# Moving a sample group's softmax one memory update earlier, and spreading its cached-value products, in a fused two-layer decoder trunk

## The chip, the core and the metric

One core of a Trainium2 chip runs the whole step in one launch. The metric is device time in microseconds (us), median over runs. The profile is one further execution, with times from the start of its span.

## The reference, cut to what matters

Two layers, each for 1024 prompt tokens and for eight samples with one new token each. Heads are of width 64: eight of group A (windowed attention), eight of group B (mLSTM matrix memory). The change touches the samples' attention over cached keys and values, three patterns of 129 positions each (128 cached, one new):

```
def dilated_gather_stats(q, k_all, v_all, window, dilation, buf_len):
    ...
    s = jnp.einsum('bthd,btjhd->bthj', q, kg) * (HEAD_DIM ** -0.5)
    m = jnp.max(s, axis=-1)
    e = jnp.exp(s - m[..., None])
    l = jnp.sum(e, axis=-1)
    o = jnp.einsum('bthj,btjhd->bthd', e, vg) / l[..., None]
    return m, l, o

def combine_by_denominators(stats):
    ...
    w = ls * jnp.exp(ms - M)
    return jnp.sum(w[..., None] * os_, axis=0) / jnp.sum(w, axis=0)[..., None]
```

The merge makes it one softmax over all 387 positions. Beside it stands the B heads' memory, updated chunk by chunk (128 tokens), for the prompt, and once for each sample:

```
def mlstm_chunk(carry, inp):
    ...
    num = iw[..., None] * jnp.einsum('bhvk,bhtk->bhtv', C, q) + jnp.einsum('bhts,bhsv->bhtv', sc, v)
    ...
    C_new = cw[..., None, None] * C + jnp.einsum('bhs,bhsv,bhsk->bhvk', ws, v, k)
```

After both come output norms, the output projection, the gated feed-forward part and the per-layer embedding.

## The kernel before, in words

Every engine has its own instruction stream, written out in order (sync, gpsimd, tensor, scalar, vector blocks). Semaphores join them: `wait_ge(*at(sem, value))` stops an engine's whole stream. No scheduler decides anything; what stands earlier runs earlier.

A layer begins with the combined input projection, done pair of heads by pair of heads (p = 0 to 7). Weights are split into a high and a low float32r part (ScalarE rounds `whi`, L1441; GpSimd subtracts `wlo` in sixteen pieces, `split`, L841), and every product is three matmuls (`three`, L888 to L890). Four pairs of A heads are attended first, while the next pair's projection fills TensorE. Then come the four **updates**, q = 0 to 3, one per pair of B heads. An update first turns q and k (`turn_qk`, L1007), broadcasts rows of gates (L1218, L1227), makes the decay matrix (VectorE L2247, ScalarE L1697), and then walks the chunks c = 0 to 7:

- TensorE: projection products of the next pair (`next_products`; none in q = 3), the state's increment (L1240), score products `kq` (L1172), output products (L1254, L1259).
- VectorE: `finish(c)` updates the state (L2287) and the output rows `yb` (L2291 to L2295); `prepare(c + 1)` weights keys and scores (L2273, L2277). In q = 3 `prepare` stands ahead of `finish`. TensorE's chunk c + 1 waits for both.
- ScalarE: evacuates projections, squares the outputs (L1647), gates of the output (L1638 to L1642). GpSimd: gates times outputs (`gated`, L860) and `split`.

At the end of an update TensorE turns the state (L1270) as soon as the last `finish` has updated it.

The samples' attention is threaded through. In q = 0 to 2 VectorE handles one of 24 groups of cached keys per chunk (`sample_keys`, L2312, L2313; group i is sample i // 3, pattern i % 3), from two key buffers in `kvb`; SyncE loads group i once group i - 2 is used (`load_keys`, L643, L644; a new sample's query row goes ahead of its first group). In q = 3 the sums are turned by TensorE (L1210), VectorE takes their maximum (`sample_max`), ScalarE the exponential (L1701), VectorE normalises (`sample_weights`), TensorE turns the weights back (`sample_turn`, L1180), and VectorE copies them to their places in `pZ` (`sample_turned`), which GpSimd has zeroed (L870). From chunk 3 on 24 value products (`sample_values`, L1191, each two instructions in the trace) run: 5, 5, 8 and 6 in chunks 3 to 6. Their values, 256 KB each, lie in the space of the spent hi part: 0 to 15 come in during q = 2 (`load_strips`, when each token tile's projection is done), 16 to 18 in q = 3 behind the samples' state (1 MB) and two blocks of weights (2 MB), 19 to 23 after a round trip of the output gates. A semaphore counts six values, so product 12 waits for values 12 to 17 and product 18 for 18 to 23. The samples' own memory (`memory_gates`, `memory_keys`, `memory_output`, `memory_update`) is VectorE's work in chunks 2 to 5 of q = 3, the first three normalised output tiles in chunk 6. TensorE then turns these tiles (L1155) and the output projection begins.

## Time and profile before

| | |
|---|---|
| median of 3 runs (lowest, highest) | 3229.04 us (3226.77, 3229.59) |
| profiled execution | 3227.93 us |
| its span | 3226.1 us |
| busy: TensorE, VectorE, ScalarE, GpSimd | 97%, 58%, 32%, 28% of the span |
| mean granted TensorE clock | 0.985 of full |
| last updates (q = 3) | about 578 to 634 us and 2167 to 2224 us |
| first updates (q = 0), chunks | about 407 to 446 us and 1997 to 2036 us |

The layers run one after the other, so each stretch appears twice. Busy time of TensorE counts its matmuls, whose ends are modelled. A wait of TensorE is lost time nearly everywhere, as the projection work behind it has to be done anyway.

### The profile page before, as it was taken

The numbers are of one execution on the slowest core, as the hardware profiler recorded it, in microseconds if no ns is written. First come the engines' busy times: TensorE is split into PE (matmuls) and PEld (weight loads), VectorE is DVE, ScalarE is ACT, GpSimd is POOL, SyncE is SP. The second block draws the span as 40 slices with busy tenths as digits, with TensorE's granted clock in tenths as the row PEclk, the third lists the DMA queues.
The fourth block names the chain that finished last, engine by engine and source line by source line (L and its number), as shares of the span: only waits on it lengthen the run. The fifth ranks groups of instructions, "written<-read, shape, count | busy, mean of one in ns | idle before, by whom it ended". The sixth has DMA issues, their size and how long they took to land.

```text
span 3226.1 us, 50829 instructions
## 1 busy us (share of the span) xinstructions
PE 3122.2 (97%) x19459; PEld 2854.5 (88%) x19459; DVE 1857.2 (58%) x4365; ACT 1028.8 (32%) x2117; POOL 891.9 (28%) x2029
## 2 busy tenths in 40 slices
PE   7999999899999999999999999999999999999999
PEld 7887777599999999999987777766999999999998
DVE  5676455755555555557477755557555555555663
ACT  4444345533111121115344433454321111111251
POOL 3111122405322333223322210332132324223231
PEclk8999999899999999999999999998999999999999
DMA  5211234612111111110221111346111111111111
GB/s 172 54 47 51 54 74 118 189 49 66 44 48 40 40 66 40 53 40 21 94 71 44 49 48 50 82 132 183 64 40 40 40 66 40 53 40 40 40 37 71
DMA packets 228570, 208.87 MB, mean 65 GB/s; under 512 B 36676, under 2 KB 207620, under 8 KB 226736
## 3 DMA queue, kind: packets, MB, share of 16 engines
q1 hardware_dynamic: 228328, 205.62, 21.3%
q8 instruction: 154, 2.52, 0.3%
q14 instruction: 88, 0.72, 0.1%
HBM read 173.96 MB, written 31.61 MB: 64 GB/s over the span
## 4 chain that ended last, share of the span: by engine, by line
PE 88%; DVE 7%; ACT 2%; issue 1%; POOL 1%; DMA 0%; SPq 0%; DVEq 0%; ACTq 0%
PE ps L888 25%; PE ps L890 24%; PE ps L889 24%; PE ps L1051 2%; PE ps L1022 2%; PE ps L1037 2%; PE ps L1191 1%; POOL wlo L841 1%; PE ps L1254 1%; PE ps L1172 1%; DVE lo L1899 1%; PE ps L1259 1%; PE ps L897 1%; DVE att L2068 1%; DVE att L2057 1%
## 5 line engine op out<-in xcount | busy, mean ns | idle before, releaser
L841 POOL TENSOR_TENSOR wlo<-raw,whi 128x128 fp32r<-128x128 f32 (+3 forms) x1952 | 857.6, 479 | 1835.4 <-ACT whi L1441 1404.3
L888 PE MATMUL ps<-hi,wlo 128*128 128x344 f32 x2880 | 927.8, 322 | 13.7 <-POOL wlo L841 8.1
L890 PE MATMUL ps<-hi,whi 128*128 128x344 f32 x2880 | 922.5, 320 | 0.0
L889 PE MATMUL ps<-lo,whi 128*128 128x344 f32 x2880 | 921.8, 320 | 0.0
L888 PEld LDWEIGHTS ps<-hi,wlo 128*128 128x128 f32 x2880 | 544.4, 189 | 16.1 <-POOL wlo L841 8.7
L890 PEld LDWEIGHTS ps<-hi,whi 128*128 128x128 f32 x2880 | 543.7, 189 | 0.0
L889 PEld LDWEIGHTS ps<-lo,whi 128*128 128x128 f32 x2880 | 542.9, 189 | 0.6
L888 PE MATMUL ps<-whi,lo 128*128 128x512 f32 (+3 forms) x1056 | 413.5, 392 | 4.9 <-POOL wlo L841 4.4
L890 PE MATMUL ps<-whi,hi 128*128 128x512 f32 (+3 forms) x1056 | 390.2, 370 | 0.0
L889 PE MATMUL ps<-wlo,hi 128*128 128x512 f32 (+3 forms) x1056 | 389.2, 369 | 0.0
L2471 DVE TENSOR_TENSOR X<-X,ps 128x344 f32<-128x344 f32 x528 | 268.5, 512 | 184.3 <-PE ps L890 182.5
L1794 ACT ACTIVATE wb<-wb 128x344 f32<-128x344 f32 x132 | 64.9, 492 | 964.8 <-DVE wb L2458 964.8
L888 PE MATMUL ps<-yhi,wlo 128*128 128x344 f32 x1056 | 339.9, 322 | 0.8 <-DVE X L2471 0.8
L890 PE MATMUL ps<-yhi,whi 128*128 128x344 f32 x1056 | 338.3, 320 | 0.0
L889 PE MATMUL ps<-ylo,whi 128*128 128x344 f32 x1056 | 337.4, 319 | 0.0
L888 PEld LDWEIGHTS ps<-whi,lo 128*128 128x128 f32 (+1 forms) x1056 | 196.9, 186 | 67.2 <-issue 28.2
L890 PEld LDWEIGHTS ps<-whi,hi 128*128 128x128 f32 (+1 forms) x1056 | 197.1, 187 | 26.6
L2450 DVE TENSOR_TENSOR wa<-ps,rstd 128x344 f32<-128x344 f32 x132 | 68.3, 517 | 258.6 <-PE ps L890 258.2
L889 PEld LDWEIGHTS ps<-wlo,hi 128*128 128x128 f32 (+1 forms) x1056 | 197.7, 187 | 20.2
L1441 ACT ACTIVATE whi<-raw 128x2048 fp32r<-128x2048 f32 (+3 forms) x106 | 188.1, 1783 | 49.0 <-DMA raw<-in_w_down 37.6
L888 PEld LDWEIGHTS ps<-yhi,wlo 128*128 128x128 f32 x1056 | 198.7, 188 | 1.5 <-DVE X L2471 1.3
L889 PEld LDWEIGHTS ps<-ylo,whi 128*128 128x128 f32 x1056 | 198.3, 188 | 0.2
(325 smaller groups left out, 3881.4 us busy)
## 6 DMA issues: line engine op xcount, KB each, us to landing
raw<-in_w_up SPq DMA_DIRECT2D x44, 1024.0 KB, 5.1
raw<-in_w_in SPq DMA_DIRECT2D x112, 256.0 KB, 4.3
raw<-in_w_down SPq DMA_DIRECT2D x22, 1024.0 KB, 4.9
kvb<-in_cache_win_k SPq DMA_DIRECT2D x48, 256.0 KB, 3.6
cache<-in_cache_win_v SPq DMA_DIRECT2D x42, 256.0 KB, 4.7
X<-x_scratch SPq DMA_DIRECT2D x4, 2064.0 KB, 12.6
raw<-in_w_out SPq DMA_DIRECT2D x8, 1024.0 KB, 8.8
raw<-in_w_ple_gate SPq DMA_DIRECT2D x8, 1024.0 KB, 5.2
```

The costliest lines, as they stand in the source:

```text
L841: pool.tensor_tensor(out=wlo[:, s, r], in0=raw[:, s, r], in1=whi[:, s, r].bitcast(F32), op=ALU.subtract).then_inc(w_split, 1)
L888: nc.tensor.matmul(out, a_lo, b_hi, start=first, stop=False)
L889: nc.tensor.matmul(out, a_hi, b_lo, start=False, stop=False)
L890: return nc.tensor.matmul(out, a_hi, b_hi, start=False, stop=last)
L897: mm = nc.tensor.matmul(ps[0:5 * NB, bank, 0:width], thin[:, a:a + 5 * NB], w_h, start=k == 0, stop=k + 1 == KT)
L1022: mm = nc.tensor.matmul(ps[:, 2 * e + a // 4, 0:(b - a) * P].rearrange("p (t n) -> p t n", n=P), q3[r, qb, :], k3[r, a:b, :], start=True, ...
L1037: mm = nc.tensor.transpose(ps[:, 4 + half, (kb % 4) * P:(kb % 4 + 1) * P], att[:, a:a + P], ident[:, :])
L1051: mm = nc.tensor.matmul(ps[HD * e:HD * e + HD, 6, 0:P], zt[:, p % 2, kb, zc:zc + HD], att[:, a:a + P], start=(kb == 0), stop=(kb == qb))
L1441: do(nc.scalar.activation(whi[:, s, 0:used], raw[:, s, 0:used], ACT.Copy), w_hi, wait=False)
L1794: do(nc.scalar.activation(w, w, ACT.Gelu_apprx_tanh), gelu_done, wait=False)
L2450: do(v.tensor_tensor(out=w[:, 2:CH + 2], in0=ps[:, s % 3, 0:CH], in1=rstd[:, col(c)], op=ALU.mult), gate_read)
L2471: do(v.tensor_tensor(out=x, in0=x, in1=ps[:, 5 + (24 * i + j) % 3, 0:CH], op=ALU.add), dn_read, wait=False)
```

## The change

1. Cached keys: twelve groups in q = 0 and twelve in q = 1, by the table `KEYS` (1, 2, 2, 2, 2, 2, 1, 0 in chunks 0 to 7); none in q = 2. SyncE's loads likewise, and value strips in q = 2 without keys between them.
2. The softmax moves to q = 2: turn of the sums and copy in chunk 0, maximum in 1, exponential in 2, weights in 3, turn back and copies in 6. TensorE waits behind both turns before its next `kq` (they share PSUM bank 0). Buffers `sm`, `zb`, `small` move to `kvb`, `pZ` to tiles 6 and 7 of lo with another layout (six copies instead of three), and GpSimd zeroes it after the first split of q = 2. The three reads of `zb` move from q = 3 to the start of q = 2.
3. Value products: two inside `turn_qk` of q = 3, four after the broadcasts, then 3, 2, 2, 3, 3, 3, 2, 0 in the chunks (table `VALUES`).
4. The samples' memory work starts one chunk earlier, its gate multiply stays in chunk 5.

```diff
-STRIPS = {2: (0, 1, 2), 3: (3,), 4: (4,), 5: (5,), 7: (6, 7)}
+KEYS = (0, 1, 3, 5, 7, 9, 11, 12, 12)
+def keys_of(q, c):
+    return range(12 * q + KEYS[c], 12 * q + KEYS[c + 1]) if q < 2 else ()
+VALUES = (6, 9, 11, 13, 16, 19, 22, 24, 24)
...
+        sm = kvb[0:HD, 0, 0:385]
+        pZ = lof[:, 6 * TOK:KT * TOK].rearrange("p (k n) -> p k n", k=2)[:, :, 0:6 * P]
...
-                    for i in range(max(2, NT * h2), NT * (h2 + 1)):
-                        load_keys(i)
-                        if h2 == PAIRS - 2:
-                            for t in STRIPS.get(i - NT * h2, ()):
-                                load_strips(t)
+                    if h2 < 2:
+                        for i in range(max(2, 12 * h2), 12 * (h2 + 1)):
+                            load_keys(i)
+                    else:
+                        sp.wait_ge(*at(kq_used, 3 * NB))
+                        for j in range(3):
+                            sp.dma_start(zb[:, j, :], Zd[j].rearrange("b (h d) -> (b h) d", d=HD)).then_inc(zb_in, 16)
+                        for t in range(NT):
+                            load_strips(t)
...
-                for j in range(3):
-                    sp.dma_start(zb[:, j, :], Zd[j].rearrange("b (h d) -> (b h) d", d=HD)).then_inc(zb_in, 16)
...
-                        pool.wait_ge(*at(gemm_done, GEMM_OUT))
-                        pool.memset(pZ, 0.0).then_inc(pz_set, 1)
...
                         split(B + n)
+                        if q + 2 == PAIRS:
+                            pool.wait_ge(*at(gemm_done, GEMM_IN + (NT + 1) * (2 * PAIRS - 1) + 6))
+                            pool.memset(pZ, 0.0).then_inc(pz_set, 1)
...
                             if half == 1 and j == 1:
+                                if p + 1 == 2 * PAIRS:
+                                    sample_values(0, 2)
...
                     next_products(done[2], ahead_b(q, 0))
+                    if q + 1 == PAIRS:
+                        sample_values(2, VALUES[0])
...
-                        if q + 1 == PAIRS and c == 2:
+                        if q + 2 == PAIRS and c == 0:
+                            pe.wait_ge(*at(kq_used, 3 * NB))
+                            for r in range(3):
+                                mm = nc.tensor.transpose(ps[0:HD, 0, (r + 1) * P:(r + 2) * P], ...)
+                            mm.then_inc(st_ready, 1)
+                        elif q + 2 == PAIRS and c == NT - 2:
                             sample_turn()
...
                         if q + 1 == PAIRS:
-                            sample_values(c)
+                            sample_values(VALUES[c], VALUES[c + 1])
                         elif c + 1 < NT:
+                            if q + 2 == PAIRS and c == 0:
+                                pe.wait_ge(*at(sp_max, 1))
+                            elif q + 2 == PAIRS and c == NT - 2:
+                                pe.wait_ge(*at(pj_done, 1))
                             kq(c + 1)
...
+                        if q + 2 == PAIRS and c == 0:
+                            sample_scores()
+                        elif q + 2 == PAIRS and c == NT - 2:
+                            sample_turned()
                         finish(c)
...
-                            sample_keys(NT * q + c)
-                        elif c == 0:
-                            sample_max()
+                            for i in keys_of(q, c):
+                                sample_keys(i)
+                            if q + 2 == PAIRS and c == 1:
+                                sample_max()
+                            elif q + 2 == PAIRS and c == 3:
+                                sample_weights()
```

**VectorE, first update, chunks 1 to 2.** `kvb<-kvb` with `att<-kvb` is one group of cached keys, `Cst` the state in `finish`. Before:

```order
L2312 TENSOR_TENSOR kvb<-kvb 128x512
L2313 TENSOR_REDUCE att<-kvb 128x8
L2287 SCALAR_TENSOR_TENSOR Cst<-Cst,cwb,ps 64x65 x2
L2291 SCALAR_TENSOR_TENSOR den<-ps,em 128x2
L2293 TENSOR_TENSOR den<-ps,den 128x2
L2294 RECIPROCAL den<-den 128x2
L2295 TENSOR_TENSOR yb<-ps,den 128x128
L2273 SCALAR_TENSOR_TENSOR att<-zt,att 128x128
L2277 SCALAR_TENSOR_TENSOR att<-ps,att 128x256
L2312 TENSOR_TENSOR kvb<-kvb 128x512
L2313 TENSOR_REDUCE att<-kvb 128x8
```

and changed:

```order
L2348 TENSOR_TENSOR kvb<-kvb 128x512
L2349 TENSOR_REDUCE att<-kvb 128x8
L2348 TENSOR_TENSOR kvb<-kvb 128x512
L2349 TENSOR_REDUCE att<-kvb 128x8
L2323 SCALAR_TENSOR_TENSOR Cst<-Cst,cwb,ps 64x65 x2
L2327 SCALAR_TENSOR_TENSOR den<-ps,em 128x2
L2329 TENSOR_TENSOR den<-ps,den 128x2
L2330 RECIPROCAL den<-den 128x2
L2331 TENSOR_TENSOR yb<-ps,den 128x128
L2309 SCALAR_TENSOR_TENSOR att<-zt,att 128x128
L2313 SCALAR_TENSOR_TENSOR att<-ps,att 128x256
L2348 TENSOR_TENSOR kvb<-kvb 128x512
```

A second group of keys now stands between `prepare` and the next `finish`.

**TensorE, opening of the last update.** `ident,zt` turns q and k, `ident,att` 64x128 turns the samples' sums, `rowr,ident` broadcasts, `rstd,kT` is `kq`, `cache,vectors` a value product. Before:

```order
L1270 MATMUL ps<-ident,Cst 64x128 x2
L1007 MATMUL ps<-ident,zt 128x128 x16
L1210 MATMUL ps<-ident,att 64x128 x3
L1218 MATMUL ps<-rowr,ident 64x512 x4
L1227 MATMUL ps<-rowr,ident 128x512 x4
L1172 MATMUL ps<-rstd,kT 128x128 x2
L1240 MATMUL ps<-zt,att 128x130
```

and changed, as far as the first chunk's products:

```order
L1295 MATMUL ps<-ident,Cst 64x128 x2
L1036 MATMUL ps<-ident,zt 128x128 x12
L1023 MATMUL ps<-cache,vectors 64x512 x2
L1036 MATMUL ps<-ident,zt 128x128 x4
L1232 MATMUL ps<-rowr,ident 64x512 x4
L1241 MATMUL ps<-rowr,ident 128x512 x4
L1023 MATMUL ps<-cache,vectors 64x512 x4
L1201 MATMUL ps<-rstd,kT 128x128 x2
L1256 MATMUL ps<-zt,att 128x130
L1201 MATMUL ps<-rstd,kT 128x128 x2
L1275 MATMUL ps<-zt,att 128x65 x2
L1280 MATMUL ps<-Cst,att 128x130
```

Six value products now stand in the opening, and the turn of the sums has left it.

## Rows read from the trace of the kernel before

**Rows 1.** VectorE's timeline in the first update: start, us, engine, line, operation, wait before.

```profile
422.06 0.69 DVE L2312 TENSOR_TENSOR kvb<-kvb 128x512 f32<-128x512 f32 x1
...
423.50 0.60 DVE L2287 SCALAR_TENSOR_TENSOR Cst<-Cst,cwb,ps 64x65 f32<-64x65 f32 x2
...
425.05 0.29 DVE L2273 SCALAR_TENSOR_TENSOR att<-zt,att 128x128 f32<-128x128 f32 x1
...
425.60 0.68 DVE L2312 TENSOR_TENSOR kvb<-kvb 128x512 f32<-128x512 f32 x1
...
427.31 0.60 DVE L2287 SCALAR_TENSOR_TENSOR Cst<-Cst,cwb,ps 64x65 f32<-64x65 f32 x2 [0.31 <-PE ps L1259]
...
432.30 0.60 DVE L2287 SCALAR_TENSOR_TENSOR Cst<-Cst,cwb,ps 64x65 f32<-64x65 f32 x2 [1.43 <-PE ps L1259]
...
445.43 0.60 DVE L2287 SCALAR_TENSOR_TENSOR Cst<-Cst,cwb,ps 64x65 f32<-64x65 f32 x2
```

**Rows 2.** TensorE's timeline at the opening of the last update, layers 0 and 1.

```profile
581.30 0.66 PE L1007 MATMUL ps<-ident,zt 128*128 128x128 f32 x4 [1.86 <-ACT rstd L1554]
...
588.12 0.80 PE L1172 MATMUL ps<-rstd,kT 64*128 64x128 f32 x4 [2.80 <-DVE att L2247]
...
2177.27 0.80 PE L1172 MATMUL ps<-rstd,kT 64*128 64x128 f32 x4 [2.78 <-DVE att L2247]
```

**Rows 3.** Windows: length; PE, PEld, DVE, ACT, POOL busy (x); clock; DMA share; GB/s.

```profile
590.00:595.00 5.00, 4.71 (x22) 3.73 (x20) 4.10 (x15) 1.56 (x6) 0.00 (x0) 0.50 0.50 45
```

**Rows 4.** The chain of work through the last update: start, us, what.

```profile
581.96 0.33 PE ps L1210 x3
...
603.30 6.36 PE ps L1191 x10
...
611.36 4.44 PE ps L1191 x10
```

**Rows 5.** VectorE's timeline in the last update, layer 0, and its end in layer 1.

```profile
613.02 2.29 DVE L2175 TENSOR_REDUCE mh<-vectors 128x32 f32<-128x2048 f32 x1
...
616.41 0.29 DVE L2273 SCALAR_TENSOR_TENSOR att<-zt,att 128x128 f32<-128x128 f32 x1
...
619.39 0.25 DVE L2183 TENSOR_SCALAR mz<-mz,mg 128x64 f32<-128x64 f32 x1
...
624.95 0.29 DVE L2273 SCALAR_TENSOR_TENSOR att<-zt,att 128x128 f32<-128x128 f32 x1
...
627.89 0.16 DVE L2199 SCALAR_TENSOR_TENSOR yt<-yrs 128x5 f32<-128x5 f32 x1
...
633.55 0.60 DVE L2287 SCALAR_TENSOR_TENSOR Cst<-Cst,cwb,ps 64x65 f32<-64x65 f32 x2 [2.23 <-PE ps L1259]
...
2223.61 0.60 DVE L2287 SCALAR_TENSOR_TENSOR Cst<-Cst,cwb,ps 64x65 f32<-64x65 f32 x2 [2.23 <-PE ps L1259]
```

**Rows 6.** Landing of the cached keys that SyncE issued at 423.9 and 427.0.

```profile
DMA to landing us min/median/max: 2.7/3.1/3.6
```

**Rows 7.** GpSimd's timeline at the third and the last update.

```profile
562.66 7.45 POOL L841 TENSOR_TENSOR wlo<-raw,whi 128x128 fp32r<-128x128 f32 x16 [1.41 <-ACT whi L1441]
...
583.36 1.37 POOL L870 MEMSET vectors<- 128x1536 f32 x1
```

**Rows 8.** TensorE's timeline in chunk 6 of the third update.

```profile
571.65 0.39 PE L1240 MATMUL ps<-zt,att 128*128 128x130 f32 x2
```

**Rows 9.** SyncE's timeline of issues at the last update, both layers.

```profile
586.40 1.80 SPq L731 DMA_DIRECT2D vectors<-z_scratch  x3
...
593.43 7.21 SPq L653 DMA_DIRECT2D vectors<-in_cache_win_v  x3
...
2182.76 5.90 SPq L653 DMA_DIRECT2D vectors<-in_cache_win_v  x3
```

**Rows 10.** Landing of value reads issued at 599.7 to 600.2, and at 611.9 to 612.6.

```profile
DMA to landing us min/median/max: 7.2/7.3/7.4
...
DMA to landing us min/median/max: 4.3/5.1/5.9
```

More of the change, by code:

```diff
@@ L505, in build, with weight_place @@
         Cs, Ct = [lof[:, j * 2048:(j + 1) * 2048].rearrange("p (v k) -> p v k", k=HD) for j in (0, 1)]
-        sm = lof[0:HD, 7168:7168 + 385]
-        pZ = lof[:, 5632:5632 + 3 * WA]
+        sm = kvb[0:HD, 0, 0:385]
+        pZ = lof[:, 6 * TOK:KT * TOK].rearrange("p (k n) -> p k n", k=2)[:, :, 0:6 * P]
+        def weight_place(i):
+            b, r = divmod(i, 3)
+            x, y, z = b // 4, b // 2 % 2, b % 2
+            a = (2 * r + x) * P + z * HD
+            return pZ[:, y, a:a + HD]
         sown = kT[0:HD, 0:WA].rearrange("p (h d) -> p h d", h=NH)
-        zb = lof[0:HD, 7760:7760 + 3 * HD].rearrange("p (s d) -> p s d", s=3)
-        small = lof[0:HD, 7960:7960 + 16]
+        zb = kvb[0:HD, 1, 0:3 * HD].rearrange("p (s d) -> p s d", s=3)
+        small = kvb[0:HD, 2, 0:16]
         sall = att[:, 3840:3840 + 3 * HD].rearrange("p (r b h) -> p r b h", r=3, b=NB)
@@ L743, in _ @@
                 sp.wait_ge(*at(yb_stored[1], 16 * last))
+                sp.wait_ge(*at(pj_back, 1))
+                sp.wait_ge(*at(pj_done, 1))
                 for t in range(3):
@@ L997, in turn_third, with sample_values @@
                     mm.then_inc(turned, 1)
+                def sample_values(first, last):
+                    for i in range(first, last):
+                        pe.wait_ge(*at(v_in[i // 6], 96))
+                        nc.tensor.matmul(ps[0:HD, 6, :].rearrange("p (k n) -> p k n", k=4), weight_place(i), value_place(i),
+                                         start=(i == 0), stop=(i == 23)).then_inc(v_used, 1)
                 def turn_qk(p):
@@ L1179, in sample_turn @@
                         for r in range(3):
-                            mm = nc.tensor.transpose(ps[:, 7, r * HD:(r + 1) * HD], sm[:, r * P:(r + 1) * P], ident[0:HD, 0:HD])
+                            mm = nc.tensor.transpose(ps[:, 0, P + r * HD:P + (r + 1) * HD], sm[:, r * P:(r + 1) * P], ident[0:HD, 0:HD])
                         mm.then_inc(pj_back, 1)
-                    def sample_values(c):
-                        if c == 3:
-                            pe.wait_ge(*at(pj_done, 1))
-                        for i in range(*((0, 5, 10, 18, 24, 24)[c - 3:c - 1])) if c >= 3 else ():
-                            b, r = divmod(i, 3)
-                            a = r * WA + b * HD
-                            pe.wait_ge(*at(v_in[i // 6], 96))
-                            nc.tensor.matmul(ps[0:HD, 6, :].rearrange("p (k n) -> p k n", k=4), pZ[:, a:a + HD], value_place(i), start=(i == 0), stop=(i == 23)).then_inc(v_used, 1)
                     if q == 0:
@@ L1205, in _ @@
                     turn_qk(p)
-                    if q + 1 == PAIRS:
-                        pe.wait_ge(*at(kq_used, 3 * NB))
-                        for r in range(3):
-                            mm = nc.tensor.transpose(ps[0:HD, 6, r * P:(r + 1) * P], sall[:, r, :, :].rearrange("p b h -> p (b h)"), ident[:, :])
-                        mm.then_inc(st_ready, 1)
                     done = (6, 10, 14) if q else (EARLY, EARLY + 2, EARLY + 4)
@@ L1710, in _ @@
                         n = B + 2 * (p + 2)
+                        if q + 2 == PAIRS and c == 2:
+                            act.wait_ge(*at(sp_max, 2))
+                            do(nc.scalar.activation(sm, sm, ACT.Exp, scale=SCALE, bias=small[:, 10:11], accum_out=small[:, 11:12]), sp_exp)
                         if q < 2 and c == 2:
@@ L1718, in _ @@
                             round_block(n + c // 6, True)
-                        if q + 1 == PAIRS and c == 2:
+                        if q + 1 == PAIRS and c == 1:
                             act.wait_ge(*at(sc_exp_in, 1))
@@ L2117, in _, with sample_scores @@
                 y_squares(PAIRS - 1, rowr[:, :], slice(4, NT))
+                def sample_scores():
+                    dve.wait_ge(*at(st_ready, 1))
+                    do(v.tensor_copy(sm[:, 0:384], ps[0:HD, 0, P:P + 384]), sp_max)
                 def sample_max():
@@ L2139, in sample_turned @@
                     dve.wait_ge(*at(pz_set, 1))
+                    wide = P + 4 * NH
                     for r in range(3):
-                        src = ps[:, 7, r * HD:(r + 1) * HD].rearrange("p (b h) -> p b h", b=NB)
-                        own = lof[:, 5632 + r * WA:5632 + r * WA + NB * (HD + NH)].rearrange("p (b x) -> p b x", b=NB)[:, :, 0:NH]
-                        do(v.tensor_copy(own, src), pj_done if r == 2 else None, wait=False)
+                        src = ps[:, 0, P + r * HD:P + (r + 1) * HD].rearrange("p (x y z h) -> p x y z h", x=2, y=2, z=2)
+                        for y in range(2):
+                            a = (6 + y) * TOK + 2 * r * P + 2 * y * NH
+                            own = lof[:, a:a + 2 * wide].rearrange("p (x w) -> p x w", x=2)[:, :, 0:2 * (HD + NH)]
+                            own = own.rearrange("p x (z v) -> p x z v", z=2)[:, :, :, 0:NH]
+                            do(v.tensor_copy(own, src[:, :, y]), pj_done if r == 2 and y == 1 else None, wait=False)
                 ig_, lf_, m0_, m1_ = (mg[:, j:j + 1] for j in range(4))
@@ L2178, in memory_output, with memory_gated @@
                     do(v.tensor_scalar(h, h, mg[:, 13:14], None, ALU.mult))
+                def memory_gated():
+                    h, y = mh[:, 0, :], mh[:, 1, :]
                     dve.wait_ge(*at(mo_in, 16))
```

20 lines of the change are left out of this document (8 added, 12 removed).

## The prediction

> **What bounds the kernel now.** I read the page first. TensorE is busy in nearly all of the span (its part 1; 97% in the table above), so a change helps only where TensorE waits or runs at its lower clock, and it hurts wherever it makes TensorE wait. Second, the order of the instructions, to see which stretches the change touches: the four updates of the matrix memory (one per pair of B heads, q = 0 to 3, each with eight chunks of tokens). In q = 0 to 2 TensorE fills every gap with projection products of the next pair. The last update, q = 3, has no such filler. Third, the timelines of VectorE and TensorE in these stretches, both layers.
>
> In the first update VectorE is nearly as full as TensorE. It idles only 0.31 us before finishing chunk 3 and 1.43 us before chunk 4 [rows 1]. One chunk costs it 1.55 us for `finish`, 0.55 us for `prepare` and 1.44 us for one group of cached keys (two instructions) [rows 1].
>
> In the last update TensorE waits 2.8 us for the decay matrix before its first score product, in both layers [rows 2], and its granted clock is at 0.50, the lower level of 1.2 GHz, while the first chunks run [rows 3]. The 24 value products then cost 6.36 us for the first five and 4.44 us for the next five [rows 4], so 0.89 us for one at full clock. Chunks go without them in 1.70 us (609.66 to 611.36). The update ends, for my purpose, when VectorE starts the last `finish`: 633.55 us in the first layer, 2223.61 in the second [rows 5].
>
> **Term 1, cached keys in two updates instead of three.** Work per key group is unchanged (1.44 us), but the first update now handles twelve, eleven of them by chunk 5 and the twelfth in chunk 6, where it handled eight. I walk VectorE through. Before, it finished the key group of chunk 1 at 423.50 and started `finish(2)` [rows 1]. Now a second group stands ahead: 424.94. From there a chunk with two groups costs 1.55 + 0.55 + 2.88 = 4.98 us, about what TensorE needs for a chunk here (4.99 us, from 427.31 to 432.30, five projection products included), but TensorE's last two chunks are shorter, and VectorE must also wait for keys. Two buffers hold the keys, so a load starts only when the group two before it is used up, and lands 2.7 us later, or 3.6 us where a new query row goes ahead of it [rows 6]. A load that starts 1.44 us before its partner is done and needs up to 3.6 + 0.4 us of issue misses its turn by about 0.45 us. That happens at groups 3, 6 and 9. So `finish(3)` starts at 424.94 + 5.42 = 430.36, `finish(4)` at 435.78, `finish(5)` at 440.75, `finish(6)` at 446.17 and `finish(7)`, after one group only, at 446.17 + 1.55 + 0.55 + 1.44 = 449.7. Before it was 445.43 [rows 1]. TensorE cannot turn the memory nor start the second update before the state is updated there, and it has no idle time behind to make this up. **+4.3 us a layer, 8.6 us in both.** Bounds: with no key waits 3 x 0.45 us less, 2.9 us a layer; if every key landed in 3.8 us, 5.8 us.
>
> The Trainium skill, "DMA: Bandwidth & Descriptors", section "Anatomy of one DMA — SWDGE (gpsimd) path", fits a transfer as 2.0 us plus its bytes over 436 GB/s, for the path that GpSimd issues. For 256 KB that is an estimate of 2.6 us, and by it every key would be in time and term 1 would be 5.8 us instead of 8.6. The rows of this trace, issued by SyncE, say 2.7 and 3.6 us, and I go by them.
>
> The second update has six projection products in a chunk instead of five, so TensorE's chunk is some 0.7 us longer. VectorE's 4.98 us fit, waits of 0.45 us too: nothing. The key groups that the third update loses lay in VectorE's idle time there: nothing gained.
>
> **Term 2, the sample softmax in the third update.** TensorE issues the three transposes of the scores (0.33 us) [rows 4] in chunk 0 and the three of the weights (0.3 us, bounded by the same row) in chunk 6, both between its own work, where it has no idle time. Behind each it waits for VectorE to empty the bank: the copy of the scores (0.55 us) runs beside 0.7 us of products, so next to nothing; the six copies of the weights, some 0.9 us, leave about 0.35 us. Sum 1.05 us a layer, 2.1 us in both. What could make it more is the zeroing of the weight places. It is now behind a split on GpSimd (7.45 us from 562.66) and takes 1.37 us [rows 7], so it ends near 571.5; TensorE arrives in chunk 6 at 571.65 plus about 1 us that it is late by then [rows 8]. It is in time by a hair. Bounds for both layers 1.3 us (no waits) to 5 us (zeroing 1.5 us late). ScalarE's exponential is some 0.8 us of its idle time in chunk 2. The zeroing and the split behind it lose nothing, since that split waited for ScalarE.
>
> **Term 3, the last update.** Two value products fill the wait in the turning of q and k, four the 2.8 us wait; with the full clock kept and the score transposes gone, the first score product goes at about 584.0 + 4 x 0.89 = 587.6 (588.12 before [rows 2]; in the second layer, where the clock fell later, 0.1 us later than before). Chunks 0, 1 and 2 with 3, 2 and 1 products: 591.0 (VectorE scales the queries until then), 593.7, 595.4, 597.2, 598.9, 599.7. The next product, number 12, waits for all of values 12 to 17. Value 17 is one of three that SyncE puts behind 3 MB of state and weights; they took it 7.21 us to issue [rows 9] and the last two landed 7.2 to 7.4 us after their issue at 599.7 and 600.2 [rows 10]. SyncE no longer issues three reads of sample rows here (1.80 us [rows 9]), so all of this comes 1.8 us sooner: value 17 lands at 599.7 + 7.4 - 1.85 = 605.2. **TensorE stands 5.5 us there**, longer than any wait that it has in this stretch now, and I take it that the clock falls. With product 12 and chunk 3 at the low clock, `finish(3)` starts at 610.4 (607.9 at full clock). From there VectorE leads: 1.55 + 3.2 (memory output, 613.02 to 616.41 less the gate) + 0.55 = 615.7; 1.55 + 5.56 (memory update, 619.39 to 624.95) + 0.55 = 623.4; 1.55 + 0.45 + 0.55 = 625.95; and 1.55 + 3.43 (three tiles normalised, 627.89 to 631.32) [rows 5] = 630.9. Value 18 waits for value 23, which lands at 612.6 + 5.9 - 1.85 = 616.65 [rows 10]; TensorE reaches it at 616.1, so this wait is hidden. Gain 633.55 - 630.9 = 2.65 us. In the second layer the three values are issued 1.1 us earlier against the first score [rows 2, 9] and the stretch before was 0.9 us longer; the same walk ends at 2218.8 against 2223.61, gain 4.8 us. **-7.5 us in both.** Bounds: full clock throughout, 4.9 and 5.9, -10.8; no value ever waited for, `finish(7)` at 625.4, -16.7; clock low after the second wait too, 1.9 and 3.1, -5.
>
> **Sum.** 8.6 + 2.1 - 7.5 = +3.2 us on the profiled execution's 3227.93 us, 3231.1. The median of the runs stands 1.1 us above that execution, so 3232.2. The bounds give -9.6 (5.8 + 1.3 - 16.7) to +11.6 (11.6 + 5 - 5).
>
> **The rivals.** *Faster: the values are there in time.* If the reads of values 12 to 17 land before chunk 2 ends, the last update is worth 16.7 us and even the late keys leave 3220 us. For it: the granted clock would stay full, and TensorE's fill is what that stretch lacks. Against it: the 3 MB ahead of them in the queue, which the change does not touch. Decides if value 17 lands before about 600 us. Chance 0.2, with every smaller mixture that ends under 3222.6.
>
> *Slower: the clock falls behind the first update.* TensorE would wait 1.7 us for chunk 7's weights and another 1.1 us before turning the memory, within 4 us. At the opening of the last update a wait of 1.9 us and one of 2.8 us some 6 us later [rows 2] are followed by the low clock [rows 3]. The dense products after that would pay what the first five value products paid against the next five, 6.36 - 4.44 = 1.9 us [rows 4], or somewhat more: +4.4 us in both layers, 3236.6; with every key as slow as 3.8 us another 3 us, 3239.6. It decides where the two waits come close enough together for the clock to drop. Against it: those waits are longer, and dense products follow at once here. Chance 0.3.
>
> *It does not do what it says: the value products do not move ahead.* Half of it is in my forecast: 12 of 24 stand behind the same landing as before. If even the first eleven were held, term 3 would be nil and the time 3239.7; the strips of hi that carry them are filled in the third update, so I give that 0.02, inside the slower case.
>
> **How the numbers follow.** My forecast, within 0.2% of no change (6.5 us, about what a measurement of this kernel tells from none), has 0.5; faster 0.2; slower 0.3. Most likely 3232 us. The range, 3220 to 3241 us, takes in both rivals' times and leaves out the rest.
>
> **What would show it.** Right: VectorE without idle time in the first update's chunks 2 to 6 and its last `finish` some 4 us later against the first score product; in the third update about 1 us more on TensorE; in the last update one wait of 4 to 6 us ahead of value product 12, released by a DMA, then the low clock for some microseconds, and the last `finish` 3 to 5 us sooner. Wrong: no lag in the first update (then the keys' groups overlap with something that I took as serial), or no DMA wait ahead of product 12 (then the forecast is too slow by up to 9 us), or the low clock in the slice behind the first update (then too fast by 4).

## The result, and the profile after

| | before | after |
|---|---|---|
| median of 5 runs (lowest, highest) | 3229.04 us (3226.77, 3229.59) | 3242.50 us (3238.04, 3242.97) |
| profiled execution, its span | 3227.93, 3226.1 us | 3242.95, 3241.2 us |
| mean granted TensorE clock | 0.985 | 0.987 |

The changed kernel is slower by 0.41% (ratio 1.0041, 95% interval 1.0026 to 1.0055), 13.5 us. That is 10.3 us more than forecast and 1.5 us beyond the range.

The page of the changed kernel: busy time of each engine, then the chain of work that ended last, by engine and by line.

```profile
PE 3128.1 (97%) x19459; PEld 2851.8 (88%) x19459; DVE 1860.4 (57%) x4371; ACT 1028.3 (32%) x2117; POOL 889.8 (27%) x2029
...
PE 84%; DVE 9%; ACT 2%; issue 1%; DMA 1%; SPq 1%; POOL 1%; DVEq 0%; ACTq 0%
PE ps L908 25%; PE ps L910 24%; PE ps L909 24%; PE ps L1080 2%; PE ps L1051 2%; PE ps L1066 2%; POOL wlo L860 1%; DMA kvb<-in_cache_win_k 1%; DVE lo L1925 1%; PE ps L1201 1%; DVE att L2094 1%; PE ps L1275 1%; PE ps L1184 1%; DVE att L2083 1%; PE ps L917 0%
```

Shares of the span say almost nothing here. One entry does: reads of cached keys (`kvb<-in_cache_win_k`) stand in the chain that sets the end. To find the microseconds I compared the start of `finish(c)` on VectorE (L2287 before, L2323 now) in both traces, chunk by chunk. How late the changed kernel is, and what each stretch adds:

| up to | layer 0: late by, added | layer 1: late by, added |
|---|---|---|
| first chunk of the first update | 2.35 | 7.62 (-2.7 since layer 0's out products) |
| last chunk of the first update | 8.70, +6.35 | 13.45, +5.83 |
| first chunk of the second update | 9.92, +1.22 | 15.96, +2.51 |
| last chunk of the third update | 10.90, +0.98 | 16.94, +0.98 |
| last chunk of the last update | 8.16, -2.74 | 12.26, -4.68 |
| sixth sum of the out products | 10.31, +2.15 | 14.16, +1.90 |

The first updates cost 12.2 us, the turns behind them 3.7, the third updates 2.0; the last updates give back 7.4; and the stretch behind the last `finish`, on which the prediction has no term, takes 4.05. The sum is 14.5 us; the profiled executions differ by 15.0, and the other 0.5 us lie between (a short fall of the clock before the first update came in layer 0 of the one execution and in layer 1 of the other).

**First update.** VectorE's timeline, layer 0, against [rows 1]: start, us, engine, line, operation, wait before.

```profile
427.31 0.60 DVE L2323 SCALAR_TENSOR_TENSOR Cst<-Cst,cwb,ps 64x65 f32<-64x65 f32 x2
...
430.21 0.69 DVE L2348 TENSOR_TENSOR kvb<-kvb 128x512 f32<-128x512 f32 x1 [0.72 <-DMA kvb<-in_cache_win_k]
...
437.43 1.02 DVE L2348 TENSOR_TENSOR kvb<-kvb 128x512 f32<-128x512 f32 x1 [0.80 <-DMA kvb<-in_cache_win_k]
...
446.93 0.99 DVE L2348 TENSOR_TENSOR kvb<-kvb 128x512 f32<-128x512 f32 x1 [0.37 <-DMA kvb<-in_cache_win_k]
...
454.13 0.60 DVE L2323 SCALAR_TENSOR_TENSOR Cst<-Cst,cwb,ps 64x65 f32<-64x65 f32 x2
```

The waits for TensorE before `finish` [rows 1] are gone: VectorE sets the pace. It waits for keys three times, 1.9 us in all. And two of the products above take 0.99 and 1.02 us where the same operation took 0.68 to 0.69 before [rows 1].

TensorE's timeline at the end of that update, and the windows behind it (columns as in [rows 3]).

```profile
452.28 0.49 PE L1256 MATMUL ps<-zt,att 128*128 128x130 f32 x2 [1.87 <-DVE att L2309]
...
454.79 0.64 PE L1295 MATMUL ps<-ident,Cst 128*64 128x128 f32 x2 [1.23 <-DVE Cst L2323]
455.07 0.78 PE L908 MATMUL ps<-whi,lo 128*128 128x512 f32 x1
```

```profile
450.00:455.00 5.00, 1.90 (x11) 1.23 (x10) 4.58 (x15) 1.09 (x5) 1.20 (x3) 0.91 0.82 233
455.00:460.00 5.00, 5.00 (x19) 4.03 (x18) 1.83 (x8) 1.50 (x5) 0.46 (x1) 0.75 0.92 233
```

TensorE worked 1.90 of the 5 us before 455 and then ran half of the next five at the lower level of 1.2 GHz, with dense products in front of it. In layer 1 the lower level lasted 6.8 us (2048.1 to 2054.9) instead of 3.4, and that turn costs 2.51 us instead of 1.22. In the trace of before the clock is 1.00 throughout there.

**Last update.** TensorE's timeline, both layers, and VectorE's last `finish` against [rows 5].

```profile
615.84 1.97 PE L1023 MATMUL ps<-cache,vectors 128*64 128x512 f32 x2 [5.28 <-DMA vectors<-in_cache_win_v]
...
2210.16 1.97 PE L1023 MATMUL ps<-cache,vectors 128*64 128x512 f32 x2 [3.72 <-DMA vectors<-in_cache_win_v]
```

```profile
641.71 0.60 DVE L2323 SCALAR_TENSOR_TENSOR Cst<-Cst,cwb,ps 64x65 f32<-64x65 f32 x2 [0.44 <-PE ps L1280]
...
2235.87 0.60 DVE L2323 SCALAR_TENSOR_TENSOR Cst<-Cst,cwb,ps 64x65 f32<-64x65 f32 x2 [0.44 <-PE ps L1280]
```

This is the wait ahead of value product 12, as forecast (5.5 us). The clock behind it, from the windows of the same trace:

```profile
610.00:615.00 5.00, 0.56 (x2) 0.00 (x0) 4.62 (x14) 2.96 (x9) 0.46 (x1) 0.95 1.09 357
615.00:620.00 5.00, 4.16 (x12) 2.10 (x12) 1.20 (x3) 0.74 (x2) 0.00 (x0) 0.50 0.85 325
```

**Behind the last update.** VectorE's and then GpSimd's timeline of the changed kernel.

```profile
649.06 6.21 DVE L2235 SCALAR_TENSOR_TENSOR yt<-yrs 128x3 f32<-128x3 f32 x1
```

```profile
641.55 6.68 POOL L860 TENSOR_TENSOR wlo<-raw,whi 128x128 fp32r<-128x128 f32 x16
...
648.55 6.70 POOL L860 TENSOR_TENSOR wlo<-raw,whi 128x128 fp32r<-128x128 f32 x16
```

An instruction on three numbers per partition lasts 6.21 us, to 655.27; GpSimd's run of sixteen splits ends at 655.25. I call this the lockout. It stands in both layers (6.18 us in layer 1). Before, the same instruction began 3.4 us into the run and took 0.36 us (VectorE's, then GpSimd's timeline of the kernel before):

```profile
640.16 0.36 DVE L2199 SCALAR_TENSOR_TENSOR yt<-yrs 128x3 f32<-128x3 f32 x1
```

```profile
636.37 0.41 POOL L860 TENSOR_TENSOR yb<-yb,zt 128x128 f32<-128x128 f32 x1 [0.58 <-ACT oa L1647]
636.74 6.91 POOL L841 TENSOR_TENSOR wlo<-raw,whi 128x128 fp32r<-128x128 f32 x16
```

Below, "tail" is the time from the start of the last `finish` to the second sum of the out products (VectorE, `add_out`): 20.2 and 20.4 us before, 22.3 and 22.3 after. TensorE needs the tiles that VectorE scales behind the long instruction, but it waits for them only 0.32 us in layer 0 and 0.36 in layer 1:

```profile
656.37 1.10 PE L1184 MATMUL ps<-ident,att 128*128 128x128 f32 x8 [0.32 <-DVE att L2248]
```

Nearly all of the rest goes with its clock. Windows over the tail of layer 0, kernel before and changed kernel (columns as in [rows 3]):

```profile
633.50:653.70 20.20, 15.65 (x96) 14.92 (x95) 14.54 (x34) 9.26 (x18) 9.56 (x23) 0.83 0.88 222
```

```profile
641.70:664.00 22.30, 17.44 (x95) 16.39 (x94) 19.07 (x34) 9.24 (x19) 13.55 (x33) 0.77 0.87 201
```

That is the lower level for 6.8 us of the tail before and for 10.2 us after, in both layers; 3.4 us more of it are 1.7 us of TensorE's work.

### The profile page after: what moved, and what is told of

It is laid out like the page before. It is cut to its first block, busy times and chain, and to the rows that moved or that the text cites. A ratio compares the mean times of both kernels' runs of the same rounds, so it can differ in the third digit from the quotient of the medians.

```text
span 3241.2 us, 50839 instructions
## 1 busy us (share of the span) xinstructions
PE 3128.1 (97%) x19459; PEld 2851.8 (88%) x19459; DVE 1860.4 (57%) x4371; ACT 1028.3 (32%) x2117; POOL 889.8 (27%) x2029
## 4 chain that ended last, share of the span: by engine, by line
PE 84%; DVE 9%; ACT 2%; issue 1%; DMA 1%; SPq 1%; POOL 1%; DVEq 0%; ACTq 0%
PE ps L908 25%; PE ps L910 24%; PE ps L909 24%; PE ps L1080 2%; PE ps L1051 2%; PE ps L1066 2%; POOL wlo L860 1%; DMA kvb<-in_cache_win_k 1%; DVE lo L1925 1%; PE ps L1201 1%; DVE att L2094 1%; PE ps L1275 1%; PE ps L1184 1%; DVE att L2083 1%; PE ps L917 0%
```

## The experiments

All kernels ran five rounds beside the kernel before, whose median was 3229.3 to 3230.0 us over these runs. The first four ask where the 13.5 us are.

**1. Keys spread out again.**

```diff
-KEYS = (0, 1, 3, 5, 7, 9, 11, 12, 12)
+KEYS = ((0, 1, 2, 3, 5, 7, 8, 9, 10), (10, 12, 14, 16, 18, 20, 22, 23, 24))
```

(`keys_of` and SyncE's loop read the row of their update.)

> The changed kernel with 10 key groups in the first update and 14 in the second instead of 12 and 12. Pile theory (VectorE is too full in the first update, TensorE waits for it and its clock falls behind the update): the first update and the turn behind it gave 6.35 and 1.2 us in layer 0, 5.85 and 2.5 us in layer 1; with two groups fewer, both put where VectorE idled 1.4 us, nearly all of the 15.9 us comes back: 3226 to 3231 us, granted clock 1.00 from 450 to 460 us. Rival (the loads of keys are slow to land, 3.5 to 3.9 us, wherever two follow each other, or the second update has no room for more): the loss stays or moves to the second update, 3238 to 3244 us.

Measured: 3229.11 us (3226.52 to 3232.58, 11 runs), ratio to before 0.9999 (0.9990 to 1.0008). The first update and the turn behind it are 7.4 and 8.2 us shorter than in the changed kernel; in the second update nothing is lost. The windows of this run:

```profile
450.00:455.00 5.00, 5.00 (x32) 4.21 (x31) 2.32 (x4) 1.41 (x3) 0.00 (x0) 1.00 1.15 309
455.00:460.00 5.00, 5.00 (x26) 3.21 (x25) 0.00 (x0) 3.16 (x11) 0.00 (x0) 1.00 1.15 98
```

Two key groups of 24 moved, and 13.4 us are back, the clock with them.

**2. The kernel before with twelve and twelve.** Its key loop takes the changed kernel's `KEYS`, and the value strips of q = 2 are issued as in the change, without keys between them; nothing else changes.

> The kernel before with nothing changed but the keys: 12 groups in each of the first two updates, none in the third; softmax and value products stay where they were. The recorded first term gives 8.6 us for both layers (3237.6 us), the ledger of the two traces 12.2 us in the first updates and 3.7 us in the turns behind them (3245 us). Rival (the loss was due to another part of the change): 3230 us or less.

Measured: 3245.08 us (3241.63 to 3250.17), ratio 1.0049 (1.0036 to 1.0061). Chunk by chunk the first updates lose 5.96 and 5.86 us, the turns 1.4 and 2.7: 15.9 in all, the ledger's figure. The clock behind the first update reads 0.93 and 0.72:

```profile
450.00:455.00 5.00, 2.33 (x15) 1.45 (x12) 4.58 (x15) 1.09 (x5) 1.09 (x3) 0.93 0.74 212
455.00:460.00 5.00, 5.00 (x18) 4.01 (x17) 1.72 (x8) 1.50 (x5) 0.46 (x1) 0.72 1.00 255
```

So the keys' table alone costs as much as the whole change lost, or more: its median is 2.6 us above the changed kernel's, but the two ranges overlap.

**3. Values 16 and 17 issued earlier.**

```diff
 sp.wait_ge(*at(gemm_done, GEMM_OUT))
+load_values(16)
+load_values(17)
 ...
-for i in range(16, 19):
-    load_values(i)
+load_values(18)
```

> The changed kernel with the loads of cached values 16 and 17 issued ahead of the memory's rows, its state and the output weights. Theory (value 17 lands at 615.8 us because it is issued last, at 607 us): it lands near 605 us, product 12 does not wait, 5.3 us per layer less; the memory's rows and state come 3.1 us later and give back 1 to 2 us on VectorE: 3233 to 3236 us. Rival (the transfers share the engines, the order does not matter): product 12 waits as long, or the memory's state holds VectorE by as much: 3240 to 3245 us.

Measured: 3246.51 us (3245.68 to 3248.85): slower than the changed kernel by 4 us, and above both ranges. TensorE's timeline:

```profile
629.09 1.97 PE L1024 MATMUL ps<-vectors 128*64 128x512 f32 x2 [9.55 <-DMA cache<-in_cache_win_v]
```

Product 12 does not wait any more. Product 18 and those behind it do, for 9.55 us (6.03 in layer 1), because their six reads count as one and five of them are issued behind the sixth, at 620.62 us. SyncE's timeline of the changed kernel shows what holds them: the store of output gates at 611.72, whose landing SyncE waits for until 619.90.

```profile
604.89 4.67 SPq L668 DMA_DIRECT2D vectors<-in_cache_win_v  x3
...
611.72 0.33 SPq L766 DMA_DIRECT2D z_scratch<-zt  x1
619.90 0.32 SPq L768 DMA_DIRECT2D mz<-z_scratch  x1
620.27 2.82 SPq L668 DMA_DIRECT2D cache<-in_cache_win_v  x5
```

The first wait had covered the second.

**4. Value products moved behind the landing.**

```diff
-VALUES = (6, 9, 11, 13, 16, 19, 22, 24, 24)
+VALUES = (6, 9, 11, 12, 12, 16, 20, 24, 24)
```

> The changed kernel with cached-value products 12 to 15 moved from the third and fourth chunk of the last update to the fifth, 16 to 19 to the sixth, 20 to 23 to the seventh. Theory (TensorE's wait of 5.3 us ahead of value product 12 holds the update, its clock falls behind it, and the thin tail costs 2 us at half clock in the first output products): the wait goes, and with it 5 us at half clock; 6 us per layer in the update and 1 us per layer behind it: 3227 to 3231 us. Rival (VectorE, or the state that it needs for the memory outputs, is next in line): no more than 3 us per layer, 3236 us or more.

Measured: 3235.81 us (3229.28 to 3239.81, 11 runs), 6.7 us faster than the changed kernel, between the two theories. The wait for value 17 is gone (4.5 us less in the last update of layer 0, 3.4 in layer 1), but a part of it has become a wait for VectorE. TensorE's timeline:

```profile
615.55 0.80 PE L1256 MATMUL ps<-zt,att 128*128 128x130 f32 x2 [3.60 <-DVE att L2309]
```

The next four try the pieces together and ask what else holds the last update.

**5. Both tables, 1 and 4.**

> Both edits together: key groups 10 and 14, and value products 12 to 23 in chunks five to seven. Taken alone they gave 13.4 and 6.7 us against the changed kernel. If the two losses are separate they add: 3242.5 - 13.4 - 6.7 = 3222 us, 3220 to 3225, and that is faster than the kernel before. Rival (both feed the same wait further on): 3226 us or more.

Measured: 3221.38 us (3216.98 to 3222.65), ratio 0.9971 (0.9961 to 0.9982). The losses add up, and this kernel is faster than the changed kernel and the kernel before.

**6. Reads in the order of their use.** The keys of 1, the change's `VALUES`, and on SyncE:

```diff
 sp.wait_ge(*at(gemm_done, GEMM_OUT))
+for i in range(16, 19):
+    load_values(i)
 ...
-load_pair(2 * PAIRS + 1)
-for i in range(16, 19):
-    load_values(i)
+load_block(B + 4 * PAIRS + 2)
+for i in range(19, 24):
+    sp.wait_ge(*at(v_used, i - 18))
+    load_values(i)
 ...
-for i in range(19, 24):
-    sp.wait_ge(*at(v_used, i - 18))
-    load_values(i)
+load_block(B + 4 * PAIRS + 3)
```

> Key groups 10 and 14, value products at their chunks as in the change, but on SyncE the cached values 16 to 18 are issued ahead of the memory's rows and values 19 to 23 ahead of the store and re-read of the output gates (which held them until 620 us), the second half of the output weights behind them. Theory (the run with only 16 and 17 moved showed that the wait of product 12 had hidden a second one, product 19's, for values 19 to 23): neither wait is left, 5 us per layer less than the 3229.1 us of key groups 10 and 14 alone: 3217 to 3221 us. Rival (from the fourth chunk on VectorE is full with the memory outputs: it was busy 4.6 to 4.8 of every 5 us in the run with the late products): only what those gave, 3221 to 3225 us. Second rival (the memory's rows and state come later and hold VectorE): 3226 us or more.

Measured: 3221.70 us (3217.36 to 3224.10, 9 runs), 0.9975 (0.9966 to 0.9985). No value is waited for, and yet it is no better than 5. The median lies only 0.7 us inside the range of the second case (VectorE is full), which the spread cannot tell from the theory's; what speaks for the second case is what TensorE waits for between 580 and 640 us (with what ended the waits: total, times, longest):

```profile
PE ps L1257 <- DVE att L2310: 5.0, 3, 3.1
```

**7. The change without its early value products.**

```diff
+VALUES = (2, 2, 2, 2, 5, 10, 18, 24, 24)
```

> The changed kernel with two value products in the opening of the last update and the rest where the kernel before has them, from the fourth chunk on (3, 5, 8 and 6). Recorded third term: the products in the opening and the first chunks are what ends the last update 2.65 and 4.8 us sooner: without them 3242.5 + 7.5 = 3250 us. Rival (the gain is the softmax that has left the opening, and the early products only run into the wait for value 17): product 12 comes 4 us later or more and its wait of 5.3 us shrinks: 3234 to 3242 us.

Measured: 3236.47 us (3233.18 to 3240.99, 11 runs): 6 us *faster* than the changed kernel. TensorE waits 2.80 us in the opening again, as before [rows 2], its clock is at 0.50 from 600 to 610 us, and the last update is still shorter than in the changed kernel, by 1.8 us in layer 0 and 0.15 in layer 1; the tail is 20.8 and 20.7 us instead of 22.3. These are 5.0 us. Another 3.7 us of the profiled execution lie where this edit changes nothing: behind both first updates TensorE waits as in the changed kernel, and yet the clock stayed at 1.00 this time. TensorE's timeline and the windows, layer 0:

```profile
450.36 0.49 PE L1256 MATMUL ps<-zt,att 128*128 128x130 f32 x2 [1.43 <-DVE att L2309]
...
452.86 0.41 PE L1295 MATMUL ps<-ident,Cst 128*64 128x128 f32 x2 [1.23 <-DVE Cst L2323]
```

```profile
450.00:455.00 5.00, 3.41 (x19) 2.83 (x20) 4.64 (x15) 1.14 (x6) 0.88 (x2) 1.00 1.03 277
455.00:460.00 5.00, 5.00 (x31) 4.28 (x30) 1.44 (x3) 1.96 (x5) 0.00 (x0) 1.00 0.89 244
```

So how much of the 6 us is the edit's own stays open. That the early products are not worth the 7.5 us of term 3 does not: even with these 3.7 us on top the time would be 10 us under its 3250. They bring nothing as the reads stand. Against the kernel before, the last updates of this run are still 4.6 and 4.8 us shorter. 2.0 of these 9.4 us lie ahead of the first `finish` (the softmax's turn has left, two value products fill the turning of q and k), the rest in the chunks, where the softmax's steps are gone and the samples' memory work starts one chunk earlier. No run has any of these alone.

**8. GpSimd's first run of splits earlier.**

```diff
-gated(q, 0, NT - 1)
+gated(q, 0, 5)
 split(B + n)
-gated(q, NT - 1, NT)
+gated(q, 5, NT)
```

> Key groups 10 and 14, and GpSimd splits the first block of the output weights after the gating of five chunks of the last update instead of seven. Theory (behind the last update a VectorE instruction on three numbers lasts 6.2 to 6.8 us, to the end of GpSimd's second run of splits, and the second output product's sum comes 2.1 us later behind the update than before): the second run begins and ends about 4 us earlier, the instruction lasts under 3 us, and 1.5 to 2 us per layer come back from 3229.1 us: 3225 to 3226.5 us. Rival (the lockout costs nothing, the 2.1 us are TensorE's half clock): the instruction is shorter and the time stays within 1 us of 3229.1 us. Second rival (the earlier run of splits slows VectorE among the memory outputs): 3230 us or more.

 

(It has the keys of 1.) Measured: 3229.45 us (3225.12 to 3233.16, 11 runs), no gain. The instruction is short (0.36 us) and the tail is 20.2 and 20.4 us: both as the theory says, 2 us a layer. But the last updates grew by 2.0 and 2.5 us. By its time this is the first rival (within 1 us of 3229.1), by what the trace shows the second: the loss moved. GpSimd's first run, now among VectorE's memory outputs, took 10.85 us instead of 6.68, VectorE's instructions beside it took longer, and TensorE waited 2.07 us for the first scaled tiles instead of 1.08, with a low clock behind it:

```profile
620.37 10.85 POOL L860 TENSOR_TENSOR wlo<-raw,whi 128x128 fp32r<-128x128 f32 x16
```

Runs 9 to 11 take the lockout away without moving the first run of splits, on three kernels. None of the three differences in time is clear of the spread by itself.

```diff
 gated(q, NT - 1, NT)
+pool.wait_ge(*at(yn_done, 4))
 split(B + n + 1)
```

**9. On the changed kernel.**

> The changed kernel, but GpSimd starts its second run of splits of the output weights only when VectorE has scaled the fourth tile behind the last update (some 1.5 us later than now). Theory (a VectorE instruction that begins within a microsecond of the start of GpSimd's run stands until the run ends; that is what makes the output products late): the instruction on three numbers lasts under 1 us, the second product sum comes 20.2 to 20.5 us after the last chunk instead of 22.3, about 2 us less per layer: 3238 to 3239.5 us. Rival (it is the thin end of TensorE's work and its half clock): 22.3 us stays and the time with it, 3241 to 3244 us.

Measured: 3241.54 us (3234.42 to 3250.93, 9 runs). VectorE's, then GpSimd's timeline:

```profile
645.78 0.15 DVE L2236 SCALAR_TENSOR_TENSOR yt<-yrs 128x3 f32<-128x3 f32 x1
```

```profile
647.06 6.94 POOL L860 TENSOR_TENSOR wlo<-raw,whi 128x128 fp32r<-128x128 f32 x16 [1.77 <-DVE att L2249]
```

The instruction takes 0.15 us; the tail is 20.2 us in layer 0 and 21.7 in layer 1. The total lies in the rival's range, but its condition, a tail of 22.3 us, is gone, so it decides nothing. The longer tail of layer 1 goes with 10.2 us at the lower clock, the one of layer 0 with 6.8. The profiled execution also shows one reason why the total spreads. In layer 1 the values' second group came late as well, a wait that the changed kernel's own profiled execution does not have, and that update took 5.5 us longer:

```profile
2222.43 1.97 PE L1024 MATMUL ps<-vectors 128*64 128x512 f32 x2 [3.19 <-DMA cache<-in_cache_win_v]
```

**10. On the kernel of run 5.**

> Key groups 10 and 14, value products 12 to 23 in chunks five to seven, and the delayed run of splits. Lockout theory: 21.7 us from the last chunk to the second product sum become 20.2 to 20.5: 3221.4 - 2.5 to 3 = 3218.5 to 3219 us. Rival: 3221 us or more.

Measured: 3219.08 us (3215.55 to 3221.22), 2.3 us less, within the spread of both; tail 19.5 and 20.2. This difference is not shown to be the lockout's: in run 5 the instruction had lasted 4.3 us, and TensorE had not waited for a tile behind it in either layer. What differs in the two profiles is the clock, at the lower level for 10.2 us in both tails of run 5 and for 3.4 and 6.8 us here.

**11. On the kernel of run 6.**

> Key groups 10 and 14, cached values and output weights in the other order on SyncE, and the delayed run of splits. Lockout theory: 21.9 us become 20.2 to 20.5, 3221.7 - 3 to 3.5 = 3218 to 3218.7 us. Rival: 3221 us or more.

Measured: 3218.11 us (3215.16 to 3220.57), 3.6 us less; tail 20.6 and 20.2. Here the trace bears the lockout out: in run 6 TensorE waited 1.51 and 1.46 us for the tiles behind it, at the same 6.8 us of lower clock, and these two waits are gone. Its ratio to the kernel before is 0.9959 (0.9947 to 0.9971). This is the lowest median of the study (run 10 is within its spread), 12 us under the kernel before (3230.0 us in its rounds) and 24 under the change.

**12. Eight and sixteen key groups.**

```diff
+KEYS = ((0, 1, 2, 3, 4, 5, 6, 7, 8), (8, 10, 12, 14, 16, 18, 20, 22, 24))
```

> The changed kernel with 8 key groups in the first update, one a chunk as before, and 16 in the second, two a chunk. If VectorE's room alone decides, the first update is 0.2 to 1 us shorter than with 10 groups, and the second, whose last two chunks had 0.4 us to spare with one group, takes 1 to 1.5 us more for its seventh: 3228 to 3231 us, the same as with 10 and 14 (3229.1 us). If the second update has no room for two groups in every chunk: 3232 us or more.

Measured: 3232.84 us (3230.44 to 3236.77, 11 runs), 3.7 us over ten and fourteen. The first update is as long as before to 0.03 us; in the second there is no room, the second case. Two groups in the seventh chunk make `finish(7)` 1.7 us late, TensorE waits for the memory's state, and in layer 0 the clock falls again. Waits of TensorE from 500 to 532 us, and a window:

```profile
PE ps L1295 <- DVE Cst L2323: 2.5, 1, 2.5
```

```profile
515.00:520.00 5.00, 5.00 (x18) 3.95 (x17) 3.50 (x8) 1.09 (x3) 0.41 (x1) 0.66 0.08 10
```

The same wait is 0.8 us in run 1, and there the clock stays. In layer 1 it is 2.57 us, and the clock stays too: the turn is 0.8 us longer than in run 1 there and 2.0 us in layer 0. One group too many in a light chunk at the end costs once for certain and can cost twice.

## Why the prediction was wrong, point by point

**Term 1: mechanism right, size off.** Forecast 4.3 us a layer, bounds to 5.8; measured 6.35 and 5.83 (5.96 and 5.86 when done alone, run 2). The walk held to the first step: `finish(2)` came 1.46 us late for 1.44 forecast. Then it ran short in two places. Key waits were 1.9 us in layer 0 instead of 3 x 0.45, since keys that follow each other closely landed in up to 3.95 us, not 3.6. And the walk took the key product at a constant 0.68 us. Five of them took 0.90 to 1.02 us, 1.3 us more in all, four of them beside GpSimd's splits and one beside a gating. The trace of before gave no warning: in its first and second updates all 14 key products beside a split took 0.67 to 0.68 us. These two make 1.85 of the 2.1 us missing in layer 0. The Trainium skill's estimate of 2.6 us for such a read, by which term 1 would be 5.8 us in both layers together, was further off than the rows.

**The slower rival came true, and I gave it 0.3.** Forecast +2.2 us a layer if the two waits came close enough together; measured 1.22 and 2.51, with TensorE's waits at 1.87 and 1.23 us for 1.7 and 1.1 forecast. The step that failed is the argument against it, that dense products follow at once: the clock fell at 454.05, before they came (455.07), and they paid. Its precedent was misread as well. In the opening of the last update before, the wait of 2.80 us began at 585.3, and the window ahead of it shows the clock already down (from 583.2 on), behind the wait of 1.86 us:

```profile
580.00:585.00 5.00, 3.70 (x23) 1.44 (x23) 2.63 (x4) 3.33 (x11) 4.73 (x9) 0.82 0.13 39
```

These waits alone do not decide it, though. Six profiles have twelve groups in the first update (the changed kernel and runs 2, 3, 4, 7 and 9), and each of their twelve turns has a wait of 1.4 to 1.9 us and one of 0.8 to 1.2 us. The clock fell in eight of them, and the turn took 1.2 to 2.7 us more; it stayed in four (both layers of run 7, layer 1 of run 4, layer 0 of run 9), with waits of 1.4 and 1.2 us as in most of the eight, and the turn took no longer than before. Of the two waits of 2.5 us in run 12 one was followed by a fall. With a wait of 0.8 to 1.0 us alone, behind the first and second updates of all runs, it never fell. What else decides it stays open. The 3.7 us of the profiled execution are thus partly luck: the mean of the twelve turns is 1.25 us a layer (an estimate from these profiles). The rival's time with slow keys, 3239.6 us, would have been the best forecast.

**Second and third update: right.** Twelve groups in the second update cost nothing (9.92 us late from its first chunk to its last). Term 2 was 1.05 us a layer, measured 0.98.

**Term 3: the sum right, the shares not shown.** -2.65 and -4.8 us forecast, -2.74 and -4.68 measured; the wait ahead of product 12 was 5.5 forecast, 5.28 measured, with the low clock behind it. But the text credits the early products with keeping the clock and skipping over the opening. Run 7 says they are worth nothing there, as they only reach the late values sooner, and run 4 that the same products behind the landing are worth 6.7 us. So the sum was met with shares that do not hold, and that much of it is luck. The faster rival had its price about right: with no value waited for (run 6) the last updates are 7.3 and 8.6 us shorter than before, 15.8 us for 16.7 forecast. Its condition failed, as the change itself does not bring value 17 before 615.8 us. Its time was mis-added, too: with the late keys, 8.6 + 2.1 - 16.7 gives 3223.0 us and not 3220.

**A missing term.** I let the last update end "for my purpose" at the last `finish`. Behind it the change took 2.15 and 1.90 us, and no term of the prediction stands for them. Two things set the tail in the fourteen profiles. One is the lockout. Where it lasts over 6 us, TensorE waits 0.3 to 2.6 us for the tile behind it; in six such cases it ends 13.5 us behind the last `finish` and the tail is 22.3 us, whatever the clock did. Where it is shorter or absent TensorE does not wait for it, and the tail goes with the clock: 19.5 us with 3.4 us at the lower level, 20.2 to 20.8 us with 6.8 to 7.9 us, 21.4 to 21.8 us with 10.2 us. In the changed kernel both came together: 0.3 to 0.4 us are TensorE's wait, and the rest goes with 3.4 us more at the lower clock. Without the lockout (run 9) the tail is 20.2 us in one layer and 21.7 in the other, so it costs 0.6 to 2.1 us a layer there; why the lower level lasts 10.2 us in some tails and 6.8 in others stays open. What makes the instruction long follows from the order on GpSimd: before, ScalarE's last square came after the first run of splits had ended, so that the second run, begun at 636.74, was 3.4 us old when VectorE came to this instruction; now the last chunks finish so close together that the first run starts with the last `finish` (641.55) instead of 4.8 us ahead of it, and the second is 0.5 us old.

**Sum.** 8.6 + 2.1 - 7.5 forecast; 12.2 + 3.7 + 2.0 - 7.4 + 4.05 measured on the profiled executions. The upper end of the range had all three terms at their bounds at once, 3240.6 us, but neither the clock behind the first update nor anything behind the last `finish`: these two make 7.8 us. Without the 4.05 us of the missing term the time would lie inside the range.

## What to carry to other kernels

When work moves to another stretch, count the engine that has to take it chunk by chunk, and leave it slack at the end of the stretch: where TensorE must wait there for the last result, a microsecond too much can cost its clock as well (it did in nine of fourteen turns here). Work moved forward is worth nothing if its data does not come forward too; look along the whole queue for the next late read before taking the first one away. Follow a moved end to where the next phase is in step again: here a small instruction came 0.5 us into another engine's long run instead of 3.4 us, and stood for 6 us. And look at more than one profile before you put a loss down to the clock: the same waits were followed by a fall in one execution and not in the next.

## What the runs showed of the hardware

The VectorE instruction of 0.15 us stands until GpSimd's run of sixteen splits ends, if it begins early in it. In seven profiles, fourteen cases, it began between 0.34 us ahead of the run and 2.46 us into it and lasted 7.05 to 4.24 us; start and duration add up to 6.7 us, the run's length, each time. In the four others where a run was under way (before, runs 2, 7 and 8), eight cases, it began 3.2 us or more into the run and took 0.15 to 0.50 us. The kernel before has a case of its own, a product at 1648.45 us (0.95 us elsewhere):

```profile
1648.45 6.07 DVE L1950 TENSOR_TENSOR rowr<-zt 128x768 f32<-128x768 f32 x1
```

The Trainium skill, "SBUF — State Buffer", section "Who interferes with whom", says that a VectorE instruction with two SBUF inputs and a GpSimd instruction that reads SBUF exclude each other, and that the second to issue blocks until the first finishes. For single instructions the traces agree: of the key products beside splits those of the changed kernel took up to 1.02 us instead of 0.68, and in the first and second updates of the kernel before, where all 14 took 0.67 to 0.68 us, the split that began just behind the product took 0.96 to 0.98 us instead of 0.45. For the lockout the size does not agree: splits follow each other every 0.42 us, and the block lasted through up to sixteen of them. Why it holds to the end of the run, and from some point between 2.5 and 3.2 us into it no longer, stays open.
